# A hybrid decoder layer on eight cores: loads, rings, mLSTM steps and output tiles moved ahead, and the latent attention's value product streaming the probabilities

## The chip, the cores and the metric

The kernel runs as one program on 8 cores of one Trainium2 chip. Each core takes one of the 8 sequences of the batch and shares nothing with the others. The metric is the device time in microseconds of the slowest core. The kernel before took 2946.66 us in the median of 3 runs (2935.18 to 2951.58).

## What is computed

Each core has `x` of 2048 tokens by 2048 channels, and 256 memory tokens. Cut to what matters:

```
h = rms_norm(x, norm)
m_qk, m_v, m_o, m_z, m_i, m_f, a_cq, a_ckv, a_kr, a_z, c_q, c_z, gates = split(h @ w_in)
# A: mLSTM, 4 heads of 256; q and k from silu(causal conv of 4 taps)
hm = rms_norm(mlstm(mq, mk / 16, mv, m_i, log_sigmoid(m_f))) * sigmoid(m_o) * silu(m_z)
# B: latent attention, 8 heads: 128 plain + 64 rotary channels, values of 128, causal
q = rms_norm(a_cq) @ w_uq;  k_nope, v = split(rms_norm(a_ckv) @ w_ukv);  k_rope = rope(a_kr)
ha = softmax(q @ k.T / sqrt(192), causal) @ v * silu(a_z)
# C: cross attention, 4 heads of 256, into 256 memory tokens
hc = softmax(c_q @ km.T / 16) @ vm * silu(c_z)
merged = sig(g_m) * (hm @ w_br_m) + sig(g_a) * (ha @ w_br_a) + sig(g_c) * (hc @ w_br_c)
out = rms_norm(x + merged @ w_out, final_norm)
```

## The kernel before

Everything is bf16 on TensorE with f32 sums. The normed input stands transposed in two tiles `hT` (tokens 0 to 1023 and 1024 to 2047). Intermediate results go to scratch tensors in DRAM (`MQT`, `MG`, `AZ`, `HAT` and so on) and are loaded from there by the stage that needs them.

**How the order comes about.** `FW.op` and `FW.dma` (L121, L132) record each instruction on its engine at once, in the order of the Python calls, with semaphore waits for what it reads and overwrites. Every engine works strictly in that order. SyncE (SP) issues all loads and stores of activations, GpSimd (POOL) all weight loads. `FW.store` (L91) puts a store on a list, and it is issued 12 TensorE instructions later (`LAG`), or earlier when its tile is to be overwritten or its tensor is read by a load whose stores are not all out. The arena hands freed memory to the next tile, which then waits for the last users of it. `mix` (L250) advances two generators so that both shares of work proceed in proportion; each `yield` tells how many matmuls' worth was done. A *dense* stream, matmuls of 512 columns from the input projection, so fills TensorE beside a *light* stream with short dependent steps.

**The stages in order.** First the norm, transposes and values (to about 166 us). Then the q and k projection with the convolution on VectorE (to about 423 us). Then the output gates of mLSTM heads 0 and 1 (`oz_block`, L698) beside `side` (L877): rotary key and gates (`ki_stream`), latent query norm (`lat_stream`), query projections (`uq_rope`, `uq_nope`). `ki_stream` reads the bias `bif`, and `oz_block` the norm weight `gmh`; both are loaded when that stage begins. The twelve `t16` tiles serve all of these, gate tiles and copies in turn (`copy_out`, L787).

Then the light stream takes `mlstm` (L902), `mla` (L1167) and `cross` (L1285), one after the other, and the dense stream `beside_mlstm` and `beside_attention`.

`mlstm` has 32 steps of 128 tokens for two heads at a time. A step is a row of small functions, spread over five phases with dense matmuls between: `sA` scores and transposes of k, `sB` weighting on VectorE (`PT` the masked scores, `kw` the weighted keys), `sC` and `sD` the state update, `sE` its copy to bf16, `sF` the output, `sG` to `sI` its norm (`hmt`), `sJ` and `sK` the transpose back. `loads` fetches `bm`, `mk`, `mq`, `mv` and `mg` of two steps.

`mla` goes over 8 heads, 4 blocks of 512 queries and, of each block, the key tiles up to the diagonal: 320 items. An item has two score matmuls (`qn` with `kn`, `qr` with `kr`), the exponential on ScalarE into `Pa`, the mask on VectorE, and up to four value matmuls. These hold 128 queries of `Pa` in the array and stream `vx`, whose 129th column gives the sum:

```python
for qt in range(q_lo, 4 * qb + 4):
    fw.op("pe", lambda e: e.matmul(bo, lhsT=P[:, jj * 128:(jj + 1) * 128], rhs=vx[:, kt, 0:129], ...
```

The four outputs of a block lie in banks 2 to 5. At its end VectorE takes each one's reciprocal (`stB`), multiplies by it and by the gate `az` into `hat`, and TensorE transposes `hat` back into `haT`. The stream stands until the whole first block of the `AZ` gates is computed (`all_az0`), and loads `az` for a head at a time.

**The end.** `gated` (L1397) computes one gate and one branch product for 128 output channels and 512 tokens, 16 + 8 matmuls. 13 of 16 shares of the first branch run in the dense stream (`first_share`); the rest, and the output projection, run alone, for the two halves of the tokens (`th`). The output projection (L1541 on) has 32 units of 16 matmuls. A unit adds its 512 columns to a tile `xo` that holds 128 rows of `x`; after four units of a tile, `finish` scales it and stores it. There are two `xo` tiles, loaded again for each pair. Between pairs 0 and 1 of the first half, the whole `HT` is loaded back into `hT[0]` (4 MB in one DMA) and `hb2` with it; `hb0` and `hb1` follow when the output weights in them are used up.

## Time and profile before

| | |
|---|---|
| median of 3 runs | 2946.66 us |
| the profiled execution | 2922.08 us |
| its span, slowest core (core 5) | 2921.0 us |
| spans of the eight cores | 2886.8 to 2921.0 us |
| mean granted TensorE clock, core by core | 0.977 to 0.981 |
| PE busy | 2707.9 us, 93% |
| PE weight loads busy | 1305.9 us, 45% |
| DVE busy | 937.9 us, 32% |
| ACT busy | 772.3 us, 26% |
| POOL busy | 399.7 us, 14% |

All are of one profiled execution, but for the first row. The span runs from the first to the last instruction of a core. Busy time is the union of an engine's instructions. Matmuls are pipelined, so the length given for one (380 ns) is not its price: a run of 16 with 512 columns takes 3.45 us. PE is TensorE's matmuls, DVE is VectorE, ACT is ScalarE, POOL is GpSimd. The kernel's slowest core is not far from the others, and both dies have the same clock.

### The profile page before, as it was taken

What the parts mean: (1) busy time and instruction counts of PE and PEld (TensorE: products, weight loads), DVE (VectorE), ACT (ScalarE), POOL (GpSimd) and SP (SyncE); (2) the same over time, 40 slices, a digit from 0 to 9 for tenths busy, and PEclk for the clock granted to TensorE, in tenths of its full rate; (3) what the DMA queues carried; (4) which work ended last, traced back from release to release, by engine and by line L of the source; (5) the groups of instructions that cost most, each with busy time, mean ns of one, the idle gap of its engine ahead of it and who ended that gap; (6) DMA issues with size and microseconds to landing.
All of it is one profiled execution on the core that took longest, in us unless ns stands there. A gap on an engine that the chain in (4) does not pass through costs nothing.

```text
span 2921.0 us, 42383 instructions; the slowest of 8 cores (2886.8 to 2921.0 us)
## 1 busy us (share of the span) xinstructions
PE 2707.9 (93%) x14237; PEld 1305.9 (45%) x14237; DVE 937.9 (32%) x1778; ACT 772.3 (26%) x1551; POOL 399.7 (14%) x566
## 2 busy tenths in 40 slices
PE   5999998988899999799999989999997899999997
PEld 2545443433444444355555544444443444444443
DVE  3455763354544433233322242111121211111123
...
GB/s 258 167 87 166 97 103 72 19 112 96 96 112 67 156 142 121 125 60 132 124 65 98 104 193 197 128 114 138 120 88 215 205 76 76 78 75 77 65 116 144
DMA packets 186580, 342.02 MB, mean 117 GB/s; under 512 B 46272, under 2 KB 140800, under 8 KB 176128
## 3 DMA queue, kind: packets, MB, share of 16 engines
...
## 4 chain that ended last, share of the span: by engine, by line
PE 80%; DMA 11%; DVE 4%; issue 2%; ACT 2%; SPq 1%; POOL 1%; DVEq 0%; ACTq 0%; POOLq 0%
PE bk L1401 21%; PE bk L460 20%; PE bk L449 13%; PE bk L1409 10%; PE bk L1559 5%; PE bk L1239 2%; PE bk L1210 2%; PE bk L1212 2%; DMA out<-m_xo 2%; DMA m_wgb<-wGB 1%; DMA ACC<-m_tmpc 1%; DMA MG<-m_t 1%; DMA m_bif<-bif 1%; DMA m_mv<-MV 1%; DMA m_cq<-CQT 1%
## 5 line engine op out<-in xcount | busy, mean ns | idle before, releaser
L460 PE MATMUL bk<-m_w,m_hT 128*128 128x512 bf16 x3072 | 731.2, 384 | 14.1 <-DVE m_t L740 10.0
L1401 PE MATMUL bk<-m_hT,m_wgb 128*128 128x512 bf16 x3072 | 708.5, 380 | 3.4 <-DMA m_wgb<-wGB 3.4
L1401 PEld LDWEIGHTS bk<-m_hT,m_wgb 128*128 128x128 bf16 x3072 | 299.0, 98 | 355.2 <-issue 7.7
L460 PEld LDWEIGHTS bk<-m_w,m_hT 128*128 128x128 bf16 x3072 | 299.8, 99 | 349.1 <-issue 31.4
L1409 PE MATMUL bk<-m_hb,m_wgb 128*128 128x512 bf16 x1536 | 369.4, 381 | 12.7 <-DMA m_hb<-HMT 7.5
L449 PE MATMUL bk<-m_hT,m_w 128*128 128x512 bf16 (+1 forms) x1600 | 366.9, 382 | 14.0 <-ACT m_t L791 7.2
L1414 DVE SCALAR_TENSOR_TENSOR m_tmpc<-m_sg,bk 128x512 f32<-128x512 f32 x160 | 109.8, 688 | 653.3 <-PE bk L1401 423.3
L1406 ACT ACTIVATE m_sg<-bk 128x512 f32<-128x512 f32 x192 | 114.8, 598 | 768.7 <-PE bk L1401 714.2
L449 PEld LDWEIGHTS bk<-m_hT,m_w 128*128 128x128 bf16 (+1 forms) x1600 | 156.7, 99 | 200.4 <-issue 27.6
L1409 PEld LDWEIGHTS bk<-m_hb,m_wgb 128*128 128x128 bf16 x1536 | 150.0, 98 | 192.1 <-issue 17.4
L1215 ACT ACTIVATE m_Pa<-bk 128x512 bf16<-128x512 f32 (+1 forms) x320 | 168.8, 534 | 248.3 <-PE bk L1212 149.3
L1239 PE MATMUL bk<-m_vx,m_Pa 128*128 128x129 bf16 x1088 | 119.4, 220 | 27.2 <-DVE m_stB L1259 22.0
L140 POOL DMA_DIRECT2D m_wgb<-wGB x96 | 53.2, 555 | 600.7 <-PE bk L1210 323.5
L1559 PE MATMUL bk<-m_wo,m_mergedT 128*128 128x512 bf16 x512 | 113.6, 382 | 20.0 <-DVE m_xo L1566 20.0
L1239 PEld LDWEIGHTS bk<-m_vx,m_Pa 128*128 128x128 bf16 x1088 | 85.5, 98 | 102.3 <-issue 44.1
L1210 PE MATMUL bk<-m_qn,m_kn 128*128 128x512 bf16 (+1 forms) x320 | 111.4, 348 | 4.1 <-ACT m_Pa L1215 3.9
L679 DVE SCALAR_TENSOR_TENSOR m_ybuf<-m_pre,m_cw,m_ybuf 128x2048 f32<-128x2048 f32 x48 | 112.9, 2351 | 5.4 <-DVE m_ybuf L676 0.5
L1559 PE MATMUL bk<-m_hb,m_mergedT 128*128 128x512 bf16 x512 | 111.8, 379 | 1.2 <-DVE m_xo L1566 1.2
L1518 POOL TENSOR_TENSOR m_mergedT<-m_acc,m_tmpc 128x512 bf16<-128x512 f32 x64 | 80.7, 1260 | 233.1 <-DVE m_tmpc L1414 233.1
L1212 PE MATMUL bk<-m_qr,m_kr 128*128 128x512 bf16 (+1 forms) x320 | 111.5, 348 | 0.0
L1569 ACT ACTIVATE m_sg<-m_xo 128x512 bf16<-128x512 f32 x64 | 40.4, 632 | 219.7 <-DVE m_xo L1566 216.8
L1146 DVE SCALAR_TENSOR_TENSOR m_t<-m_t,bk 128x512 bf16<-128x512 f32 x64 | 43.9, 687 | 147.0 <-PE bk L460 91.4
...
## 6 DMA issues: line engine op xcount, KB each, us to landing
m_wgb<-wGB POOLq DMA_DIRECT2D x96, 768.0 KB, 7.7
m_w<-wA POOLq DMA_DIRECT2D x16, 2048.0 KB, 19.7
m_xt<-x SPq DMA_DIRECT2D x16, 1024.0 KB, 12.9
m_xo<-x SPq DMA_DIRECT2D x16, 1024.0 KB, 5.6
out<-m_xo SPq DMA_DIRECT2D x15, 1024.0 KB, 5.8
m_w<-wMEM POOLq DMA_DIRECT2D x4, 2048.0 KB, 16.8
...
m_accl<-ACC SPq DMA_DIRECT2D x16, 512.0 KB, 7.0
```

The costliest lines, as they stand in the source:

```text
L449: fw.op("pe", lambda e: e.matmul(bk[0:M, 0:n], lhsT=w[:, kc, c0:c0 + M], rhs=src(kc, tb * 512, n), start=(kc == 0), stop=(kc == KC - 1)), ...
L460: fw.op("pe", lambda e: e.matmul(bk[:, 0:ncols], lhsT=src(kc, tt * 128, 128), rhs=w[:, kc, 0:ncols], start=(kc == 0), stop=(kc == KC - 1)) ...
L679: fw.op("dve", lambda e: e.scalar_tensor_tensor(out=yb[:], in0=pre[:, tap:tap + S], scalar=cw[:, j, tap:tap + 1], in1=yb[:], op0=ALU.mult, ...
L1210: fw.op("pe", lambda e: e.matmul(bs[:, 0:ncols], lhsT=kn[:, kc_], rhs=qn[:, q0:q0 + ncols], start=True, stop=False), reads=[kn.r, qn.r], w ...
L1212: fw.op("pe", lambda e: e.matmul(bs[:, 0:ncols], lhsT=kr[:, kc_], rhs=qr[:, q0:q0 + ncols], start=False, stop=True), reads=[kr.r, qr.r], w ...
L1215: fw.op("act", lambda e: e.activation(out=P[:, 0:ncols], in_=bs[:, 0:ncols], func=AF.Exp, scale=SC), reads=[r_bs], writes=[P.r])
L1239: fw.op("pe", lambda e: e.matmul(bo, lhsT=P[:, jj * 128:(jj + 1) * 128], rhs=vx[:, kt, 0:129], start=(kt == 0), stop=(kt == qt)), reads=[P ...
L1401: fw.op("pe", lambda e: e.matmul(gb[:, 0:512], lhsT=w[:, kc, :], rhs=h0[:, kc, tcs], start=(kc == 0), stop=(kc == 15)), reads=[w.r] + h0.r ...
L1406: fw.op("act", lambda e: e.activation(out=sg, in_=gb[:, 0:512], func=AF.Tanh, scale=0.5), reads=[r_gb], writes=[r_sg])
L1409: fw.op("pe", lambda e: e.matmul(rb[:, 0:512], lhsT=w[:, 16 + kc, :], rhs=hb[:, kc, tcs], start=(kc == 0), stop=(kc == 7)), reads=[w.r, hb ...
L1414: fw.op("dve", lambda e: e.scalar_tensor_tensor(out=o[:], in0=sg, scalar=1.0, in1=rb[:, 0:512], op0=ALU.add, op1=ALU.mult), reads=[r_sg, r ...
L1559: fw.op("pe", lambda e: e.matmul(bk[:, 0:512], lhsT=mT[:, kc, t8 * 128:(t8 + 1) * 128], rhs=wv[:, kc, :], start=(kc == 0), stop=(kc == 15) ...
```

## The change

- `store` takes a lag of its own and keeps its list sorted by due time.
- `bif` and `gmh` are allocated and loaded in the convolution stage, after the second projection block's second tile (`early_loads`).
- The output gates get a ring of their own, `g16` (6 tiles of 256 columns, lag 28). `t16` has 11 tiles, and 8 from the last dense block beside the mLSTM on.
- In the mLSTM `kw` goes ahead of `PT`; `sG` moves to the end of its own step, `sH` and `sI` a phase earlier, `loads` two phases earlier; a second `loads` stands at the start. A phase counts 3.61 rather than 3.53.
- The `AZ` gates are computed channel by channel instead of token by token (`az_block`), so `AZ` lies transposed, and a head waits only for its own tiles.
- In `mla` the value matmul holds 128 keys of `vx` in the array and streams up to 512 queries of `Pa`; the output comes out transposed, in banks 2 and 3 in turn. The sums are added up on VectorE (`sumP`), split into two bf16 parts (`hi`, `lo`), and summed over the partitions by two matmuls with `twos`. One row of the result goes to DRAM (`DEN`), comes back as 32 x 16 (`dn`) for the reciprocal, goes out again (`REC`) and comes back on all partitions (`rec`), and GpSimd multiplies. This is the generator `closing`, which goes on over 11 items beside the next block. Scores run 3 items ahead, not 2, on four banks.
- The output projection gets four `xo` tiles with a semaphore entry per 512 columns, a table of hooks that says after which unit each load is issued, and `HT` in 8 pieces.

```diff
+        def early_loads():
+            fw.dma("sp", bif[:], bif_d, writes=[bif.r])
+            fw.dma("sp", gmh[:], gmh_d, writes=[gmh.r])
...
+                if h == 1 and ci == 1:
+                    early_loads()
...
-        t16s, nxt_t16 = mk("t16", 12, [128, 512], BF16)
+        t16s, nxt_t16 = mk("t16", 11, [128, 512], BF16)
+        g16s, nxt_g16 = mk("g16", 6, [128, 256], BF16)
...
             loads(0)
+            loads(1)
...
                 if ok(t - 1):
                     sD(t - 1, 1)
-                    sG(t - 1)
+                    sH(t - 1)
                 if ok(t):
                     sA(t)
                 yield 1
                 if ok(t - 1):
-                    sH(t - 1)
                     sE(t - 1, 1)
                 if ok(t):
                     sB(t)
-                yield 1
                 if ok(t - 1):
                     sI(t - 1)
+                    if t % 2 == 0 and 0 < t and t + 2 < N:
+                        loads(t // 2 + 1)
+                yield 1
...
                     sE(t, 0)
-                    if t % 2 == 0 and t + 2 < N:
-                        loads(t // 2 + 1)
+                    sG(t)
...
+            def closing(h, qb, acc, u):
+                k = 4 * h + qb
+                hi, lo = nxt_hi(), nxt_lo()
+                fw.op("act", lambda e: e.copy(out=hi[:], in_=acc[:]), reads=[acc.r], writes=[hi.r])
+                fw.op("dve", lambda e: e.tensor_tensor(out=lo[:], in0=acc[:], in1=hi[:], op=ALU.subtract), reads=[acc.r, hi.r], writes=[lo.r])
+                yield 3
+                bd, r_bd = q_banks()
+                for part in (hi, lo):
+                    fw.op("pe", lambda e: e.matmul(bd[:, 0:512], lhsT=twos[:], rhs=part[:], start=(part is hi), stop=(part is lo)),
+                          reads=[twos.r, part.r], writes=[r_bd])
+                rec = nxt_rec()
+                fw.op("act", lambda e: e.copy(out=rec[0:1, :], in_=bd[0:1, 0:512]), reads=[r_bd], writes=[rec.r])
+                fw.store(DEN_d[k:k + 1, :], rec[0:1, :], reads=[rec.r], to=m_DEN[k])
+                yield 3
+                dn = nxt_dn()
+                fw.dma("sp", dn[:, 0:16], DEN_d[k:k + 1, :].rearrange("o (p c) -> (o p) c", c=16), reads=[m_DEN[k]], writes=[dn.r])
+                yield 3
+                fw.op("dve", lambda e: e.reciprocal(out=dn[:, 16:32], in_=dn[:, 0:16]), reads=[dn.r], writes=[dn.r])
+                fw.store(REC_d[k:k + 1, :].rearrange("o (p c) -> (o p) c", c=16), dn[:, 16:32], reads=[dn.r], to=m_REC[k])
+                yield 1
+                fw.dma("sp", rec[:], REC_d[k:k + 1, :].partition_broadcast(128), reads=[m_REC[k]], writes=[rec.r])
+                yield 1
+                haT = nxt_haT()
+                fw.op("pool", lambda e: e.tensor_tensor(out=haT[:], in0=u[:], in1=rec[:], op=ALU.mult), reads=[u.r, rec.r], writes=[haT.r])
+                fw.store(HAT_d[h * 128:(h + 1) * 128, qb * 512:(qb + 1) * 512], haT[:], reads=[haT.r], to=m_HA[qb // 2])
...
+                if kt == 0:
+                    while h not in az_heads:
+                        yield 1
+                    az = nxt_az()
+                    fw.dma("sp", az[:], AZ_d[h * 128:(h + 1) * 128, qb * 512:(qb + 1) * 512], reads=[m_AZ[h]], writes=[az.r])
...
+                fw.op("pe", lambda e: e.matmul(bo[:, off:512], lhsT=vx[:, kt, :], rhs=P[:, 0:ncols], start=(kt == 0), stop=(kt == last)),
+                      reads=[P.r, vx.r], writes=[r_bo])
...
+                    fw.op("dve", lambda e: e.tensor_tensor(out=acc[:, off:512], in0=acc[:, off:512], in1=P[:, 0:ncols], op=ALU.add),
+                          reads=[P.r, acc.r], writes=[acc.r])
...
+                    fw.op("dve", lambda e: e.tensor_tensor(out=u[:], in0=bo[:, 0:512], in1=az[:], op=ALU.mult), reads=[r_bo, az.r], writes=[u.r])
...
+            for u, t8 in ((0, 2), (0, 3), (9, 4), (10, 5), (17, 6), (18, 7)):
+                at(u, x_load, xos[t8 % 4], th * 8 + t8)
+            if th == 0:
+                for q in range(8):
+                    at(2 + 3 * q, h0_piece, q)
+                for i in range(4):
+                    at(14 + 4 * i, fetch_gb, 48 + i)
+                at(26, load_hb, hb0, 0, 1)
+                at(28, load_hb, hb1, 1, 1)
...
+            if th == 0:
+                ar.free(xos[2:])
+                del xos[2:]
+                hb2 = ar.alloc("hb", [128, 8, 1024], BF16)
+                load_hb(hb2, 2, 1)
```

How the change moves instructions is shown at three places. A number at a row's start only counts rows.

VectorE in the mLSTM, one step (rows with `m_t` are the dense stream's gate evictions). Before:

```order
439 L998 SCALAR_TENSOR_TENSOR m_Cf<-m_Cf,m_eb,bk 128x257 x2
440 L1030 TENSOR_SCALAR m_stM<-m_stM 128x2
441 L1033 SCALAR_TENSOR_TENSOR m_stM<-m_stM 128x2
442 L970 TENSOR_TENSOR m_PT<-bk,m_DT 128x256
443 L976 TENSOR_SCALAR m_kw<-bk,m_WS 128x256 x2
444 L705 SCALAR_TENSOR_TENSOR m_t_3430<-m_t_3430,bk 128x256
445 L707 SCALAR_TENSOR_TENSOR m_t_3430<-m_t_3430 128x256
446 L709 TENSOR_TENSOR m_t_3438<-m_t_3430,m_gmh 128x256
447 L1042 SCALAR_TENSOR_TENSOR m_hmt<-bk,m_stM,m_mg 128x256 x2
```

and now:

```order
439 L1012 SCALAR_TENSOR_TENSOR m_Cf<-m_Cf,m_eb,bk 128x257 x2
440 L1044 TENSOR_SCALAR m_stM<-m_stM 128x2
441 L1047 SCALAR_TENSOR_TENSOR m_stM<-m_stM 128x2
442 L721 SCALAR_TENSOR_TENSOR m_t_3435<-m_t_3435,bk 128x256
443 L723 SCALAR_TENSOR_TENSOR m_t_3435<-m_t_3435 128x256
444 L725 TENSOR_TENSOR m_g_3450<-m_t_3435,m_gmh 128x256
445 L988 TENSOR_SCALAR m_kw<-bk,m_WS 128x256 x2
446 L991 TENSOR_TENSOR m_PT<-bk,m_DT 128x256
447 L1056 SCALAR_TENSOR_TENSOR m_hmt<-bk,m_stM,m_mg 128x256 x2
```

`kw` stands ahead of `PT`, the statistics `stM` a phase before them, and `hmt` directly behind `PT`, with no eviction between.

SyncE's DMAs in the attention, one head change, where `kn` to `vx` are the next head's. Before:

```order
414 L140 DMA HAT<-m_haT 128x1024
415 L140 DMA m_kn<-KNT 128x2048
416 L140 DMA m_qn<-QNT 128x2048
417 L140 DMA m_qr<-QRT 64x2048
418 L140 DMA m_vx<-VA 128x16x128
419 L140 DMA m_az<-AZ 128x16x128
420 L140 DMA CZ<-m_t_3434 128x512
```

and now:

```order
454 L144 DMA DEN<-m_rec 1x512
455 L144 DMA m_kn<-KNT 128x2048
456 L144 DMA m_qn<-QNT 128x2048
457 L144 DMA m_qr<-QRT 64x2048
458 L144 DMA m_vx<-VA 128x16x128
459 L144 DMA m_dn<-DEN 32x16
460 L144 DMA CZ<-m_t_3439 128x512
461 L144 DMA DEN<-m_rec 1x512
462 L144 DMA REC<-m_dn 32x16
463 L144 DMA m_rec<-REC 128x512
464 L144 DMA m_dn<-DEN 32x16
465 L144 DMA HAT<-m_haT 128x512
```

Between the head's loads and the dense stream's stores (`CZ`) now stand the small DMAs of two closings.

GpSimd from the end of the mLSTM on; `m_w` and `m_wgb` are weights. Before:

```order
232 L1035 TENSOR_TENSOR m_stM<-m_stM,m_mhalf 128x2 x2
233 L140 DMA m_w<-wA 128x8192 x2
234 L140 DMA m_wgb<-wGB 128x3072 x20
235 L1515 TENSOR_TENSOR m_acc<-m_accl,m_tmpc 128x512 x2
```

and now:

```order
232 L1049 TENSOR_TENSOR m_stM<-m_stM,m_mhalf 128x2
233 L144 DMA m_w<-wA 128x8192
234 L1277 TENSOR_TENSOR m_haT<-m_u,m_rec 128x512 x6
235 L144 DMA m_w<-wA 128x8192
236 L1277 TENSOR_TENSOR m_haT<-m_u,m_rec 128x512 x8
237 L144 DMA m_wgb<-wGB 128x3072 x4
238 L1277 TENSOR_TENSOR m_haT<-m_u,m_rec 128x512 x9
```

The weight loads stood together with nothing between; now each group comes after multiplications of earlier blocks.

## Rows read from the trace of the kernel before

**Rows 1.** Stretches: us, busy time (and instructions) of each engine, PEclk, DMA share, GB/s

```profile
690.00:1182.00 492.00, 446.02 (x2457) 221.74 (x2458) 215.93 (x515) 190.17 (x503) 99.32 (x149) 0.98 0.51 111
1182.00:1680.00 498.00, 463.52 (x3064) 247.19 (x3063) 140.38 (x484) 208.21 (x391) 6.96 (x13) 0.98 0.45 101
...
2150.00:2300.00 150.00, 121.27 (x547) 53.69 (x545) 37.74 (x39) 22.88 (x63) 11.71 (x33) 0.92 0.67 197
```

**Rows 2.** Timeline, gates' start: start, us, what; in brackets the idle time before

```profile
459.23 0.68 ACT L734 ACTIVATE m_gif<-bk,m_bif 8x512 f32<-8x512 f32 x1 [28.33 <-DMA m_bif<-bif]
...
462.34 8.00 PE L460 MATMUL bk<-m_w,m_hT 128*128 128x512 bf16 x28 [10.03 <-DVE m_t L740]
```

**Rows 3.** PE's waits from 600 to 690 us: us in total, times, longest

```profile
PE bk L449 <- ACT m_t L791: 10.5, 1, 10.5
```

**Rows 4.** Pieces of the chain that ended last: start, us, what

```profile
629.97 30.12 DMA MG<-m_t
...
973.01 15.53 DMA m_bm<-BH
...
1195.89 14.60 DMA AZ<-m_t
...
1226.06 0.23 PE bk L1239 x4
...
2304.52 3.45 PE bk L1401 x16
...
2791.44 110.52 PE bk L1559 x512
```

**Rows 5.** PE's waits in the mLSTM, from 690 to 1182 us

```profile
PE bk L986 <- DVE m_kw L976: 15.2, 12, 2.5
PE bk L449 <- ACT m_t L791: 7.2, 4, 5.5
PE bk L1051 <- DVE m_hmt L1042: 6.5, 6, 2.2
PE bk L986 <- DMA m_mv<-MV: 4.1, 1, 4.1
PE bk L986 <- DVE m_Cf L998: 4.1, 3, 3.4
```

**Rows 6.** PE's waits in the attention, from 1182 to 1680 us

```profile
PE bk L1239 <- DVE m_stB L1259: 22.0, 24, 15.3
PE bk L1210 <- ACT m_Pa L1215: 3.9, 8, 0.6
PE bk L1239 <- DVE m_hat L1261: 3.7, 12, 0.3
```

**Rows 7.** Groups by form: busy us, mean ns of one, idle before

```profile
L1146 DVE SCALAR_TENSOR_TENSOR m_t<-m_t,bk 128x512 bf16<-128x512 f32 x64 | 43.9, 687 | 147.0 <-PE bk L460 91.4 <-PE bk L1239 26.0 <-PE bk L1272 10.9
```

**Rows 8.** DMAs issued from 1315 to 1335 us: KB each, us to landing

```profile
m_wgb<-wGB POOLq DMA_DIRECT2D x4, 768.0 KB, 30.5
m_w<-wA POOLq DMA_DIRECT2D x1, 2048.0 KB, 17.9
...
CZ<-m_t SPq DMA_DIRECT2D x2, 128.0 KB, 16.8
```

**Rows 9.** The same of the whole execution, median landing

```profile
out<-m_xo SPq DMA_DIRECT2D x15, 1024.0 KB, 5.8
...
AZ<-m_t SPq DMA_DIRECT2D x32, 128.0 KB, 1.8
...
m_vx<-VA SPq DMA_DIRECT2D x8, 512.0 KB, 9.5
...
m_hb<-HMT SPq DMA_DIRECT2D x2, 2048.0 KB, 9.4
```

**Rows 10.** PE's waits from 2150 to 2300 us

```profile
PE bk L1559 <- DVE m_xo L1566: 21.2, 3, 17.6
PE bk L1409 <- DMA m_hb<-HMT: 7.5, 1, 7.5
```

283 lines of the change are left out of this document (150 added, 133 removed).

## The prediction, made before the change was run

> **What bounds the kernel now.** I read the table of stages first. Its columns to look at are PE's busy time against the stretch and the granted clock: TensorE is busy 446 of 492 us while the mLSTM runs, 464 of 498 us during the latent attention, and only 121 of 150 us in the output projection of the first half, at a clock of 0.92 [rows 1]. Nothing else comes near a stage's length: VectorE is busy 140 us of the attention's 498. So time can only come from TensorE's idle stretches, and for each I looked up what ended it.
>
> At the gates' start ScalarE waits 28.33 us for the 8-element bias `bif`, and TensorE stands for 10.03 us. The 28 matmuls after that take 8.00 us [rows 2], where 16 of them take 3.45 at full clock [rows 4], so 28 should take 6.0: a long stop costs some 2 us more at half clock. I charge these 2 us wherever PE stops for long.
>
> In the query projection PE waits 10.5 us once for ScalarE's `t` tile [rows 3]; the chain names the `MG` store that holds the tile, 30.12 us long [rows 4].
>
> In the mLSTM the waits are many and small: 15.2 us for `kw`, 6.5 for `hmt`, 7.2 for an eviction, 4.1 for `mv` and 4.1 for the state [rows 5]. The eviction's longest wait stood behind the load of `bm`, 15.53 us [rows 4].
>
> At the attention's start one wait of 15.3 us ends with VectorE's first reciprocals [rows 6]; the chain shows the `AZ` store of 14.60 us behind it [rows 4]. Over the stage the block ends cost 22.0, 3.9 and 3.7 us, that wait included [rows 6]. In the output stage PE waits 21.2 us for `xo` tiles and 7.5 for `hb` [rows 10]. The same 512 matmuls of the second half run in 110.52 us without a stop [rows 4].
>
> **The change part by part.**
>
> *Early `bif` and `gmh`.* Both loads go ahead of the last queue of weights, into the conv stage, which has time. That takes away 10.0 + 2.0 = **12 us** (bounds 8 and 12; nothing new is waited for).
>
> *Own ring for the gate tiles, lag 28.* The `t16` ring loses its 64 gate tiles to `g16` and has 11 buffers left for the copies. The 30 us in which stores land late [rows 4] stay, since two weight loads are under way. A copy comes every 1.7 us (4 of its matmuls and 4 of the gates', 8/16 of 3.45), so 11 buffers last 19 us where 12 shared ones last 17. I take **3 us** of the 10.5 (bounds 0 and 10).
>
> *mLSTM.* `kw` goes ahead of `PT`, and the statistics, `hmt` and the loads a phase or two earlier. `kw` gains one VectorE operation only, but has no statistics of the same phase before it: I take 9 of 15.2. `hmt` has a whole phase more: 6 of 6.5. The loads stand two phases earlier, some 6 us (492 us in 165 phases), against waits of 5.5, 4.1 and 3.4 at most: 10 of these 13. Together **25 us**. The bounds are 0 (the evictions of the dense stream, which stand between these steps, hold them as before) and the whole 37 [rows 5].
>
> *Attention's start.* Each head waits only for its own four tiles of `AZ`, and the mLSTM's share of the mix grows from 3.53 to 3.61, so head 0's tiles are long stored: 15.3 + 2 = **17 us** (bounds 12 and 17).
>
> *Block ends.* With the sums streamed over 512 queries there are two output banks in turn, so PE need not wait for evictions: (22.0 - 15.3) + 3.9 + 3.7 = **14 us**. The transposes go too, see the work.
>
> *TensorE's work.* 1088 value matmuls at 0.23/4 us are 62.6 us [rows 4], and 128 transposes of as many columns each are 7. In their place stand 320 matmuls with 139264 columns, which at 3.45 us for 16 x 512 are 58.6, and 64 matmuls for the denominators, 13.8. Net **3 us more**. So streaming by itself saves nothing: weight loads were hidden already.
>
> *VectorE.* 296 running additions of up to 512 columns, and two more operations a block, at 0.69 us at most [rows 7] some 230 us, less 80 us of the old ones. VectorE goes from 140 to 290 us of 498. That lies beside TensorE and costs nothing while it isn't held up.
>
> *The denominators' way.* This is the new wait. Each of 32 blocks makes four DMAs in a row: `DEN` out, `dn` in, `REC` out, `rec` in. VectorE's reciprocal stands three items behind the load of `dn`, 4.5 us (498/320 = 1.5 us an item). An undisturbed small store lands in 1.8 us, so mostly it is there in time. Behind the next head's `vx` it is 9.5 us [rows 9], 5 us too late seven times. But during weight loads small stores landed after 16.8 us, with the loads themselves at 17.9 and 30.5 [rows 8]. VectorE is strictly in order: behind a waiting reciprocal stand the additions that free `Pa` tiles, the masks and the evictions of the dense stream's two banks. A dense unit takes 3.45 us and about as much again of the attention's work, so I let PE outlast some 5 us. POOL now has its multiplications between the weight fetches, which therefore come in three separate groups inside the attention: one 2 MB, one 2 MB, and four of 768 KB together with `hb`. A single one would hold VectorE 17.9 - 4.5 = 13 us at worst; I take 11, so PE 6 and 2 for the clock. The last I take at 22 of 26 us, so PE 17 and 2. Sum 8 + 8 + 19 = **35 us** more. Bounds: 2 (all meet a moment between closings) and 160 (below).
>
> The Trainium skill, page "DMA: Bandwidth & Descriptors", section "Queues, rings and completion order", says that each DMA engine takes turns between the queues, packet by packet, so that a small transfer on one queue has to wait for little of a large one on another. By it these stalls would be near 2 us, and the sum 33 us lower. The trace bears it out badly: behind the weights, issued on another queue, the 128 KB stores took nine times as long as alone [rows 8, 9].
>
> *Output tiles.* Four `xo` buffers, loaded 6 to 8 units of 3.45 us before their use, and `HT` in eight pieces rather than 4 MB in one that blocks the queue. All 28.7 us go, with two half-clock stretches 33. Late next is `hb2`: its load now waits for the stores of the last two tiles. Such a store was issued about 6 us after its tile's last matmul, by the steps of `finish`, and lands in 5.8, and 2 MB of `hb` need 9.4 more [rows 9], 21 us with nothing else under way; it is wanted after four gated blocks of 24 matmuls (5.18 us each) and 16 matmuls more, 24 us. I take 3 us. Gain **30 us** (bounds 20 and 33).
>
> **The sum.** -12 - 3 - 25 - 17 - 14 + 3 + 35 - 30 = **-63 us**. The profiled execution took 2922.1 us, of which 2921.0 are the span, so it would take 2859. It lies 24.6 us under the median of the runs shown, 2946.66, and I take the difference from that: **2884 us**.
>
> **The rivals.**
>
> *A, the round trips stay hidden* (2 in place of 35): 2946.7 - 96 = 2851 us. For it: undisturbed landings of 1.8 us, and `u` and `rec` have two buffers, so only the reciprocal and `u`'s `az` tile can hold VectorE. Against it stand the late stores [rows 8]. The Trainium skill's rule, above, would give this case. Chance 0.27.
>
> *B, the mLSTM keeps its waits* (5 in place of 25) and the round trips cost 50: 2946.7 - 28 = 2919 us. For it: VectorE's rows between the steps of the mLSTM are evictions, and those did not move. Chance 0.13.
>
> *C, slower: the reciprocal holds VectorE at every block.* The place is the wait for `dn`; the price is 5 us of PE in each of 32 blocks, 160 in place of 35: 2884 + 125 = 3009 us. It decides once `dn` lands more than 4.5 + 5 = 9.5 us after its issue as a rule, which is what the landing behind `vx` shows [rows 9]. SyncE is in order too: a `dn` load waits there until `DEN` has landed, and a `rec` load until `REC` has, with stores and head loads queued behind. Against it: of the blocks only one in four stands right behind a head's loads. Chance 0.08.
>
> **How the numbers follow.** My forecast has 0.52. The range from 2830 to 2942 us runs from A with all 37 us of the mLSTM (about 2839, and some spread of the runs, 2935 to 2952 before) to B with the round trips at 70; C and the ends of the others, 2 in 10, are left out. A measurement of this kernel can tell about 0.5%, 14.7 us, from no change. Under 2932 us lie all of A, nearly all of the forecast and two thirds of B: 0.86. Within 0.5% on both sides 0.07, slower 0.07, nearly all C.
>
> **What would show it.** PE's wait at the gates' start gone, and `m_gif` not behind `bif`. In the mLSTM's stretch the five waits [rows 5] at 12 us rather than 37, with `kw` under 8. At the attention's start no wait over 3 us. In the attention two to four stops of PE of 5 to 20 us that end with VectorE, each at a time of weight loads, with `m_dn` or `m_az` as the last releaser; none there would mean A, one at every block C. The 512 output matmuls of the first half in some 112 us, and a stop of a few us at the second half's first use of `hb2`. If the attention's stage lost nothing and the mLSTM's waits only changed their names, the gain would be right by accident.

## The result, and the profile after

The changed kernel took 2978.98 us in the median of 20 runs (from 2944.91), the kernel before 2945.14 in as many beside it. The ratio is 1.0091, with a 95% interval of 1.0053 to 1.0128: **slower by 0.9%**, where 2884 us and 86% for faster had been forecast. (The two medians are of all runs; in the ratios and in the experiments' times, runs in which one half of the chip, cores 0 to 3 or 4 to 7, was held at a lower clock are left out, and for e5 to e8, where almost none would be left, I give the mean core span of the halves that were not held, against 2911.3 us for five such halves of the kernel before.)

The profiled execution has a span of 2943.7 us (before 2921.0), on core 5 again. Cut at the same instructions in both, it splits as follows:

| stretch | before, us | after, us | difference |
|---|---|---|---|
| norm, convolution | 423.7 | 420.4 | -3.3 |
| gates, query projections | 267.0 | 270.2 | +3.2 |
| mLSTM | 504.1 | 496.8 | -7.3 |
| latent attention | 481.6 | 545.7 | **+64.1** |
| cross attention | 96.5 | 101.6 | +5.1 |
| dense work up to the output, first half | 378.3 | 375.7 | -2.6 |
| output, first half | 133.8 | 114.4 | -19.4 |
| dense work, second half | 506.3 | 498.3 | -8.0 |
| output, second half, and end | 129.8 | 120.5 | -9.3 |

The stretches that answer to [rows 1], with the same columns:

```profile
690.00:1187.00 497.00, 457.30 (x2519) 227.18 (x2520) 218.53 (x517) 190.71 (x505) 99.73 (x150) 0.97 0.54 113
1187.00:1733.00 546.00, 453.55 (x2111) 208.09 (x2109) 281.85 (x581) 234.19 (x446) 47.00 (x43) 0.91 0.43 101
2210.00:2325.00 115.00, 112.97 (x516) 50.67 (x515) 35.42 (x38) 22.46 (x62) 11.57 (x33) 0.99 0.84 238
```

The attention has fewer matmuls than before and takes longer, at a mean granted clock of 0.91 where it was 0.98. That mean is not one level but two: pieces at half clock among others at full clock, such as these after the first stop:

```profile
1203.00:1206.00 3.00, 3.00 (x9) 1.03 (x7) 0.21 (x1) 1.32 (x3) 0.00 (x0) 0.50 0.00 0
1207.00:1240.00 33.00, 33.00 (x164) 15.66 (x163) 21.97 (x42) 19.21 (x36) 2.53 (x2) 1.00 0.47 109
```

By the trace's clock record, the stretch has 14 such pieces of 3.4 to 13.7 us, 92.9 us in all, where before had 17.1. The output stage has lost its idle time.

One thing has to be known before stretches are compared. The dense stream is mixed in by counts, and the change altered the counts. Between the first score matmul and the cross attention's first, the traces have 1140 dense matmuls of 512 columns before (764 + 256 + 120) and 1084 now (512 + 240 + 224 + 108); the 56 others stand elsewhere, 44 of them in the dense stretch behind the cross attention and 12 in the mLSTM's. At 3.45 us for 16 they are 12.1 us. So for the same work the attention is not 64 but some 76 us longer. Of the 64.1, TensorE's idle time makes 58.3 (34.2 before, 92.5 now) and its busy time 5.8. By the forecast's own +3 us for the attention's matmuls and the 12.1 us fewer dense ones, the busy time should have fallen by 9, so my estimate of what the half clock cost is 15 us.

TensorE's waits in the attention, which answer to [rows 6], are these (in us: total, times, longest):

```profile
PE bk L1262 <- DVE m_dn L1271: 35.0, 7, 5.6
PE bk L1262 <- DVE m_Pa L1249: 18.7, 2, 10.2
PE bk L1317 <- DMA m_vx<-VA: 10.1, 1, 10.1
PE bk L1262 <- ACT m_hi L1257: 6.1, 3, 3.4
PE bk L1262 <- DVE m_lo L1258: 4.8, 3, 3.0
PE bk L1317 <- DVE m_Pa L1249: 4.2, 1, 4.2
PE bk L1470 <- DVE m_tmpc L1475: 2.8, 1, 2.8
```

L1262 is the pair of denominator matmuls. Together these make 81.7 us, against 29.6 in [rows 6]. One more ends the stretch, the first load of the cross attention (before, 1.2 us):

```profile
PE bk L1368 <- DMA m_cq<-CQT: 10.9, 1, 10.9
```

SyncE had issued that load only at 1729.9 us, right after a store of `haT` for which it had waited 7.2 us.

The releaser in these rows is put down to the instruction that VectorE finished last, so one has to ask what VectorE itself waited for, and then what SyncE waited for:

```profile
DVE m_dn L1271 <- DMA m_dn<-DEN: 57.2, 14, 10.3
DVE m_u L1336 <- POOL m_haT L1277: 34.3, 7, 5.6
...
DVE m_u L1336 <- DMA m_az<-AZ: 29.7, 3, 12.5
```

```profile
SPq L77 <- POOL m_haT L1277: 140.7, 32, 7.2
SPq L77 <- DMA REC<-m_dn: 70.5, 32, 14.3
SPq L77 <- DVE m_dn L1271: 55.5, 28, 5.9
SPq L77 <- DMA DEN<-m_rec: 39.0, 20, 7.1
```

Two things show. The seven waits of 35 us have their like in VectorE's seven waits for GpSimd's `haT`: a block's `u` overwrites that of two blocks earlier, which the multiplication at the end of that block's closing has yet to read. And SyncE stands 306 us of 546 for steps of the closings, with the `az` loads behind them. (The 306 us are no price: in e4 below, which has no way through DRAM, SyncE stands 339 us of 483.) One such piece, from the timeline (start, length, engine; idle time before in brackets):

```profile
1306.11 0.59 POOL L144 DMA_DIRECT2D m_w<-wA  x1 [7.88 <-PE bk L1244]
...
1308.01 1.68 SPq L144 DMA_DIRECT2D REC<-m_dn  x1
1321.57 0.34 SPq L144 DMA_DIRECT2D m_rec<-REC  x1
...
1323.82 0.38 PE L1262 MATMUL bk<-m_hi,m_twos 128*128 128x512 bf16 x1
1325.50 1.25 POOL L1277 TENSOR_TENSOR m_haT<-m_u,m_rec 128x512 bf16<-128x512 f32 x1 [18.80 <-DMA m_rec<-REC]
1326.88 0.34 SPq L144 DMA_DIRECT2D HAT<-m_haT  x1
1327.75 0.44 SPq L144 DMA_DIRECT2D m_az<-AZ  x1
1331.27 0.69 DVE L1336 TENSOR_TENSOR m_u<-bk,m_az 128x512 f32<-128x512 f32 x1 [11.68 <-DMA m_az<-AZ]
1332.71 0.59 PE L1262 MATMUL bk<-m_lo,m_twos 128*128 128x512 bf16 x1 [8.51 <-DVE m_Pa L1249]
```

A 2 MB weight load starts on GpSimd's queue. The 2 KB of `REC`, issued on SyncE's 2 us later, have SyncE wait 11.8 us, until 1321.57 (of the 32 such stores one more took over 7 us, 14.6 us from 1441.5 on, 14 us after four weight loads had been issued); then comes `rec`, the multiplication, the store of `haT`, and only then the `az` load of the current block. VectorE's `u` waits for it, `lo` stands behind `u`, and TensorE is 8.5 us late. The reciprocal has no part in this stop.

Outside the attention two waits took the place of removed ones. At the gates:

```profile
426.46 0.29 POOL L815 TENSOR_SCALAR m_Mneg<-m_maskf 128x128 f32<-128x128 f32 x1 [66.94 <-ACT m_cosT L675]
426.88 0.57 POOL L144 DMA_DIRECT2D m_w<-wKI  x1
...
434.66 1.89 PE L457 MATMUL bk<-m_hT,m_w 128*72 128x512 bf16 x4 [13.24 <-DMA m_w<-wKI]
```

The wait for `bif` [rows 2] is gone. But with `gmh` allocated earlier, the small mask `Mneg` was given the place of a tile that ScalarE still read for the cosine. GpSimd waits there, and the weights `wKI` behind it come 34 us later than before (393.0 us). In the mLSTM, against [rows 5]:

```profile
PE bk L457 <- DVE m_t L1177: 14.7, 2, 12.4
PE bk L1000 <- DVE m_kw L988: 11.1, 9, 3.3
PE bk L969 <- ACT m_hmo L1073: 3.8, 1, 3.8
```

`hmt` and `mv` are waited for no longer, the state for 1.2 rather than 4.1 us, `kw` for 11.1 rather than 15.2, and a new wait of 12.4 us is an `AZ` gate tile's: the `t16` ring, cut to 8 just there, is full of stores that land late behind a weight load.

### The profile page after: what moved, and what is told of

The parts are those of the page before. It is cut to its first block, busy times and chain, and to the rows that moved or that the text cites. A ratio compares the mean times of both kernels' runs of the same rounds, so it can differ in the third digit from the quotient of the medians.

```text
span 2943.7 us, 41762 instructions; the slowest of 8 cores (2900.3 to 2943.7 us)
## 1 busy us (share of the span) xinstructions
PE 2719.1 (92%) x13405; PEld 1278.0 (43%) x13405; DVE 1083.3 (37%) x1881; ACT 802.1 (27%) x1615; POOL 440.2 (15%) x598
## 4 chain that ended last, share of the span: by engine, by line
PE 76%; DMA 15%; DVE 3%; issue 2%; POOL 1%; SPq 1%; ACT 1%; DVEq 0%; POOLq 0%; ACTq 0%
PE bk L1462 20%; PE bk L468 16%; PE bk L457 16%; PE bk L1470 10%; PE bk L1638 8%; DMA m_dn<-DEN 3%; DMA REC<-m_dn 2%; DMA m_rec<-REC 2%; PE bk L1242 1%; PE bk L1244 1%; PE bk L1317 1%; DMA DEN<-m_rec 1%; DMA QNT<-m_t 1%; SPq L144 1%; DMA m_wgb<-wGB 1%
## 5 line engine op out<-in xcount | busy, mean ns | idle before, releaser
L468 PE MATMUL bk<-m_w,m_hT 128*128 128x512 bf16 x2560 | 616.3, 387 | 1.5 <-DVE m_Gt L839 1.5
L457 PE MATMUL bk<-m_hT,m_w 128*128 128x512 bf16 (+1 forms) x2112 | 494.0, 384 | 37.6 <-DVE m_t L1177 14.7
L468 PEld LDWEIGHTS bk<-m_w,m_hT 128*128 128x128 bf16 x2560 | 251.4, 99 | 285.6 <-issue 22.0
L457 PEld LDWEIGHTS bk<-m_hT,m_w 128*128 128x128 bf16 (+1 forms) x2112 | 207.3, 99 | 284.2 <-issue 60.5
L1325 DVE TENSOR_TENSOR m_sumP<-m_sumP,m_Pa 128x512 f32<-128x512 f32 (+3 forms) x264 | 159.1, 603 | 11.7 <-ACT m_Pa L1247 0.3
L1317 PE MATMUL bk<-m_Pa,m_vx 128*128 128x512 bf16 (+1 forms) x320 | 114.7, 359 | 14.2 <-DMA m_vx<-VA 10.1
L1277 POOL TENSOR_TENSOR m_haT<-m_u,m_rec 128x512 bf16<-128x512 f32 x32 | 41.0, 1281 | 483.0 <-DMA m_rec<-REC 390.4
L720 ACT ACTIVATE m_t<-bk 128x512 f32<-128x512 f32 x64 | 38.2, 597 | 209.3 <-PE bk L468 199.8
## 6 DMA issues: line engine op xcount, KB each, us to landing
ACC<-m_tmpc SPq DMA_DIRECT2D x32, 256.0 KB, 11.2
```

Of the source, the lines that this page charges most:

```text
L457: fw.op("pe", lambda e: e.matmul(bk[0:M, 0:n], lhsT=w[:, kc, c0:c0 + M], rhs=src(kc, tb * 512, n), start=(kc == 0), stop=(kc == KC - 1)), ...
L468: fw.op("pe", lambda e: e.matmul(bk[:, 0:ncols], lhsT=src(kc, tt * 128, 128), rhs=w[:, kc, 0:ncols], start=(kc == 0), stop=(kc == KC - 1)) ...
L1317: fw.op("pe", lambda e: e.matmul(bo[:, off:512], lhsT=vx[:, kt, :], rhs=P[:, 0:ncols], start=(kt == 0), stop=(kt == last)), reads=[P.r, vx ...
L1325: fw.op("dve", lambda e: e.tensor_tensor(out=acc[:, off:512], in0=acc[:, off:512], in1=P[:, 0:ncols], op=ALU.add), reads=[P.r, acc.r], wri ...
```

## The experiments

Edits are against the changed kernel, unless they say before. Ratios are to the kernel before on the same chip; "attention" is the length of that stretch in the profiled execution, on its slowest core if none is named.

### Which part costs

**e1** takes the old `mla` and the old `AZ` gates back; **e2** puts only the new ones into the kernel before.

```diff
-            yield from az_block(0, d2_banks)
+            yield from gate_block(I_AZ[0], AZ_d, 0, m_AZ[0], d2_banks)
+            all_az0.append(True)
...
```

> The kernel after with the attention and the AZ gates of before; early loads, rings, mLSTM steps and output tiles stay changed. Theory S (the loss of the change is made inside the attention): its stretch goes back from 546 to about 482 us, the wait of about 15 us for the first reciprocals returns within it, and the whole takes about 64 us less than after: ratio to before 0.985 to 0.992. Rival M (the loss comes from moved arena places and from SyncE's and GpSimd's order, wherever it shows): under a third of the 64 us comes back, ratio over 1.0.

> The kernel before with the new attention and the transposed AZ gates only. Theory S: it loses what e1 gains, about 55 to 65 us, ratio to before 1.019 to 1.022, with the gap between the two denominator matmuls (hi to lo) at some 60 us in total. Rival M: the new attention alone costs under 20 us, ratio under 1.007, and most of the loss of after comes only with the other parts.

e1: 2883.51 us, ratio **0.9817** (0.9789 to 0.9846), attention 483 us. e2: 2981.5 us, **1.0158** (1.008 to 1.0235), attention 534. Theory S holds, and more than expected: without the new attention the change is 1.8% faster. The attention costs 46 us alone (e2, 23 to 69), 64 in its own stretch, 76 there for the same work, and some 80 as the difference of after and e1.

**e8** puts only the output projection's changes into the kernel before, **e14** only the mLSTM's order and 3.61, **e16** only the early loads.

> The kernel before with the output projection's changes alone (four xo tiles with an entry per 512 columns, the table of hooks, HT in eight pieces, hb2 behind). The prediction had 30 us for it (28.7 of waits, two half-clock stretches, less 3 for hb2). In after the stages from the first output projection on were shorter by 19.4 + 8.0 + 9.3 = 36.7 us, of which 9.3 after the last matmul. Theory: the same here, ratio 0.986 to 0.989. Rival: part of that came from the four-way last tile or from other changed places, and alone it gives under 25 us, ratio over 0.991.

The mean span is 2869.8 us (5 halves) against 2911.3 for before. That is -41 us, **0.986**: the theory holds.

> The kernel before with the new order of the mLSTM steps and the phase count of 3.61 only. The prediction had 25 us for it (waits of 37 us down to 12), with 0 as the bound if the dense stream's evictions between the steps hold them as before. In after the stretch was 7.3 us shorter, with a stop of 12.6 us in it that came from the shortened t16 ring. Theory O (the order gives its 25 us, the ring took part of it back): ratio to before 0.991 to 0.994 and the five waits together at 12 to 17 us. Theory N (most waits changed their names only): 0.995 to 0.999, lost time of TensorE in the stretch at 60 us or more against 71.7 before.

0.9992 (0.9954 to 1.0029), nothing. Between the two profiles the stretch shrank by 14.0, 11.2 and 6.6 us on cores 0, 1 and 3 (on core 1 with `kw` at 10.9 and `hmt` at nothing), but the three stretches behind it, up to the output, grew by 11.1, 12.8 and 18.8 us. Over all eight cores the means are -8.4 and +11.0 us. The waits did not only change their names, so N's mechanism is not it; its number comes close, since what was gained there was lost behind. The count of 3.61 has a small part in that: it moves 16 dense matmuls, 3.4 us, out of the attention (1140 to 1124) and behind the cross attention, which makes nothing longer as a whole. But in the attention TensorE's idle time also grew, from a mean of 32.4 to 40.6 us, and no run shows why.

e16's edit:

```diff
+        gmh = ...; bif = ...; Mneg = ...    # ahead of the rotary tables' tiles
+                if h == 1 and ci == 1:
+                    early_loads()
```

> The kernel before with bif and gmh loaded in the convolution stage as in the change, and with Mneg there too, so that GpSimd's queue isn't held as it was in after; no other ring. The prediction had 12 us for the early loads (bounds 8 and 12), and after showed no gain: the wait for wKI (13.4 us) stood where that for bif (10.2) had been. Theory P: with the queue free the 12 us are there, ratio 0.995 to 0.997. Rival: as in e12 against e1 (0.9819 and 0.9817), where the wait of 14.2 us went and the whole took as long; then 0.998 to 1.001.

0.9977 (0.9937 to 1.0018), -7 us in the middle: not told apart from nothing, nor from the 12 us of theory P. The gates' stretch itself did get shorter, from a mean of 266.0 us over the eight cores to 257.5.

**e7** moves `Mneg` the same way in the changed kernel.

> The kernel after with the mask tile Mneg allocated and filled in the convolution stage, ahead of the rotary tables' tiles. In after GpSimd stands 66.9 us before it, because its place was that of a tile which ScalarE still read for the cosine, and the load of wKI stands behind it, issued at 426.9 us instead of 393.0 in before; TensorE then waits 13.4 us for wKI. Theory P (a moved arena place holds GpSimd's queue, and that is all the gates' stage lost): the 13 us wait goes, nothing comes in its place, norm to gates together 12 to 15 us shorter, ratio to before 1.003 to 1.006. Rival (another wait stands behind it, for gmh or for the two weights): under 5 us, ratio 1.007 to 1.012.

No stop at `wKI` is left, and the gates' stretch is 259 us rather than 270 (core 0). The mean span is 2927.7 us (7 halves), 1.006 to before. Theory P, as far as this goes; its number is at the edge.

### Which wait of the closings costs

**e3**:

```diff
-            us, nxt_u = mk("u", 2, [128, 512], F32)
+            us, nxt_u = mk("u", 4, [128, 512], BF16)
```

> The kernel after with four u tiles in bf16 (4 KB) in place of two in f32 (4 KB), so that a block's product u need not wait for GpSimd's multiplication of the block two before; all DMAs and the reciprocal stay where they are. Theory U (VectorE is held by the u ring: 34 us of waits for GpSimd's haT, seven times, once a head): the seven stops of TensorE of 4 to 6 us before the matmul of lo go, 35 us of the 60.6, the two of 9 to 10 us that stand behind a late az load stay; ratio to before about 0.997 (after: 1.009). Theory D (VectorE is held by the reciprocal that waits for dn, as rival C of the prediction had it): nothing changes, 1.009 within 0.003.

1.0006 (0.9979 to 1.0033): a gain of 25 us on the changed kernel, where theory U had 35. The seven stops are gone, theory U holds for them. But VectorE's waits for `dn` grew:

```profile
DVE m_dn L1271 <- DMA m_dn<-DEN: 103.2, 24, 10.1
DVE m_u L1336 <- DMA m_az<-AZ: 31.5, 3, 12.0
```

**e4** computes the same with no way through DRAM:

```diff
-                rec = nxt_rec()
-                fw.op("act", ... copy(out=rec[0:1, :], in_=bd[0:1, 0:512]) ...)
...
+                rec = nxt_rec()
+                fw.op("dve", lambda e: e.reciprocal(out=rec[:], in_=bd[:, 0:512]), reads=[r_bd], writes=[rec.r])
+                yield 1
```

> The kernel after with no way through DRAM: VectorE takes the reciprocal of the denominators straight from the bank, on all 128 partitions (128x512), right behind the two matmuls, and GpSimd multiplies an item later. The four DMAs of a block are gone. Theory Q (SyncE's order is what costs: behind a DEN, REC or rec that waits, az and head loads and stores stand): all of the 60.6 us between the two denominator matmuls go but for a few, less what the reciprocal takes; at 0.7 us a piece, as other 128x512 operations, the attention's stretch is about 480 us and the ratio to before 0.987 to 0.990. If the reciprocal is dear (over 3 us a piece, 96 us of VectorE in all), VectorE holds TensorE again and the ratio stays over 1.0. Theory W (the running sums' 190 us of VectorE are what costs, not the closings): the stretch stays over 520 us either way.

There are two runs, 2889.32 and 2892.69 us, against 2929.11, the median of seven of before: about 0.987, with no interval. The attention takes 483 us. The reciprocal is dear, and the sentence on that case is wrong:

```profile
L1265 DVE RECIPROCAL m_rec<-bk 128x512 f32<-128x512 f32 x32 | 107.3, 3353 | 5.0 <-PE bk L1262 4.9
```

```profile
1185.00:1668.00 483.00, 427.72 (x2048) 199.67 (x2088) 390.78 (x581) 216.14 (x413) 49.24 (x43) 0.96 0.42 97
```

VectorE is busy 391 us of 483 and doesn't bound: TensorE waits 4.1 us for the new reciprocal. The work beside TensorE is harmless here; waits for a DMA, in order, are not. Theory W falls. (This stretch holds 1064 dense matmuls, 20 fewer than after's, 4.3 us: without the closings' long tail fewer are mixed in.)

**e5** (four `u`, and the 32 x 16 reciprocal as a power of -1 on GpSimd), **e6** (four `u`, and `az` loaded a block ahead) and **e9** (both) take the other holders away.

```diff
-                fw.op("dve", lambda e: e.reciprocal(out=dn[:, 16:32], in_=dn[:, 0:16]), ...
+                fw.op("pool", lambda e: e.tensor_tensor(out=dn[:, 16:32], in0=dn[:, 0:16], in1=mone[:], op=ALU.pow), ...
```

```diff
+                    if k + 1 < 32 and (k + 1) // 4 in az_heads:
+                        load_az(k + 1)
```

> As e3 (four u tiles in bf16), and the 32x16 reciprocal is taken by GpSimd (a power of -1) rather than by VectorE, so that VectorE never waits for dn; all four DMAs of a block stay, in SyncE's order. In e3 VectorE waited 103 us for dn in 24 places, up to 10.1 each, and TensorE still stood some 45 us longer in the attention than in e4. Theory D2 (that rest is VectorE behind dn, seen as late m_hi): most of it goes, the stretch falls from 528 to about 490 us and the ratio to before to about 0.988. Theory Q2 (it is SyncE, where az and head loads stand behind DEN, REC and haT): under a third goes, stretch over 512, ratio over 0.995, and the stops behind m_az stay.

> As e3, and the az tile of a block is loaded at the start of the block before, in the same two buffers. Theory Q2: the two stops of 9 us before lo (at about 1320 and 1450 us) and the one of 6.8 beside the second go, some 20 to 25 us, ratio 0.992 to 0.994. Theory D2: the reciprocal still waits and holds VectorE at the same places, so under 8 us go, ratio 0.998 to 1.001.

> e5 and e6 together: four u tiles, the reciprocal on GpSimd, and az a block ahead. The round trip through DRAM stays with its four DMAs. e5 and e6 gave nothing each, and in their traces the wait only changed its name: without dn on VectorE it waited 84.8 us for az, with az early it waited 130.4 us for dn. Theory B (the closings cost only by what they hold on VectorE, and each holder hides the other): with both away the attention's stretch is 480 to 495 us, as in e4 (483), ratio to before 0.985 to 0.990. Theory T (the round trip costs in itself, by SyncE's order for the head loads, the dense stream's stores and the rings, or by GpSimd's 2.9 us for each power): the stretch stays over 515 us, ratio over 0.995.

e5: 2947.6 us (3 halves), 1.012, attention 560 (core 5). e6: 2913.9 us (5 halves), 1.001, attention 529 (core 5). e9: **1.015** (1.0096 to 1.0204), attention 569. The theories with a gain (D2 in e5, Q2 in e6, B in e9) fell; in e6 it came out as D2 had it, no gain and VectorE held by `dn`. e6's stops behind `az` did go, and others came, behind `hi` (43.8 us, 14 times): I take it for the same VectorE, now late through `dn`. One row of each tells it, of e5 (core 5), of e6 (core 5) and, of e9, ScalarE's and TensorE's:

```profile
DVE m_u L1338 <- DMA m_az<-AZ: 84.8, 7, 21.7
```

```profile
DVE m_dn L1278 <- DMA m_dn<-DEN: 130.4, 25, 12.1
```

```profile
ACT m_rec L1274 <- POOL m_haT L1286: 112.7, 11, 14.7
...
PE bk L1251 <- ACT m_rec L1274: 70.5, 10, 11.4
```

With VectorE free of both, ScalarE is held: its copy of the sums goes into one of two `rec` tiles, and the exponentials stand behind it.

**e13** gives e9 rings of three for `u` (e9 has four), `dn` and the sums, which get tiles `den` of their own; `rec` stays at two, and these tiles and `DEN` and `REC` are bf16, for room. And **e15** issues e13's closing DMAs and the `haT` stores on GpSimd.

```diff
-                rec = nxt_rec()
-                fw.op("act", lambda e: e.copy(out=rec[0:1, :], ...
+                den = nxt_den()
+                fw.op("act", lambda e: e.copy(out=den[:], ...
```

```diff
-                fw.dma("sp", dn[:, 0:16], DEN_d[k:k + 1, :] ...
+                fw.dma("pool", dn[:, 0:16], DEN_d[k:k + 1, :] ...
```

> e9 with rings that outlast a closing at every place where an engine writes: the row of denominators gets its own ring of three tiles (den, bf16) in place of the two rec tiles, rec is written by its load only, dn and u have three tiles; DEN and REC lie in bf16. In e9 VectorE was free of both holders and ScalarE stood instead, 112.7 us in 11 places, for GpSimd's multiplication that reads rec, TensorE 70.5 us behind it. Theory R (what costs is the in-order engine held by a ring of two against a round trip longer than a short block; with rings of three none is held): no stop of TensorE over 5 us between 1200 and 1690 us, stretch 478 to 495 us, ratio 0.985 to 0.991. Theory T (the round trip itself costs through SyncE's queue, where it holds head loads and the dense stream's stores): the stops come back under further names (m_t of the dense stream, m_qn, m_kn), stretch over 515, ratio over 1.0.

> e13 with the four DMAs of the round trip and the store of haT issued by GpSimd, so that SyncE's queue holds nothing of the closings; the trip stays the same. In e13 SyncE stood 362 us of 567 for haT, dn, DEN and REC, and VectorE 63 us for az and 49 us for stores of tmpc behind it. Theory T (SyncE's order carries the trip's waits to all other loads and stores): the waits for az and for ACC end, stretch 475 to 495 us, ratio to before 0.983 to 0.991. Rival G (the same in GpSimd's order: its weight fetches wait behind the closings instead, or the trip's length itself holds VectorE on u): stretch over 510 us, with waits of TensorE for m_w or m_wgb, ratio over 0.998.

e13: **1.0177** (1.0084 to 1.027), attention 567 us on the slowest core. Rings aren't enough; SyncE stands as before, and `az`, a whole block ahead, comes up to 24.2 us late. From e13, SyncE's waits and one of VectorE's:

```profile
SPq L77 <- POOL m_haT L1288: 153.1, 31, 14.2
SPq L77 <- POOL m_dn L1281: 122.8, 32, 7.2
SPq L77 <- DMA DEN<-m_den: 44.0, 24, 6.5
SPq L77 <- DMA REC<-m_dn: 42.4, 32, 4.8
```

```profile
DVE m_u L1351 <- DMA m_az<-AZ: 63.4, 5, 24.2
```

e15: **1.0312** (1.0253 to 1.0371), attention 577 to 595 us over the cores. SyncE no longer waits for the trip, and `az` comes in time, but now GpSimd takes every landing, its 2.9 us power and the multiplication one after the other, and VectorE waits for the `u` ring of three:

```profile
DVE m_u L1351 <- POOL m_haT L1288: 170.5, 18, 27.8
```

That is rival G's second form: the length of the trip itself. So e15 says nothing on SyncE alone. **e17** is e4 with `u` in bf16 and one `rec` tile; **e18** adds the four DMAs, of a row that nobody reads (edit against e17):

```diff
+                fw.store(DEN_d[k:k + 1, :], rec[0:1, :], reads=[rec.r], to=m_DEN[k])
...
+                fw.dma("sp", dn[:, 0:16], DEN_d[k:k + 1, :] ..., reads=[m_DEN[k]], writes=[dn.r])
+                yield 3
+                fw.store(REC_d[k:k + 1, :] ..., dn[:, 0:16], reads=[dn.r], to=m_REC[k])
+                yield 1
+                fw.dma("sp", jr[:], REC_d[k:k + 1, :].partition_broadcast(128), reads=[m_REC[k]], writes=[jr.r])
```

> The partner of e18, on the same chip: e4 (reciprocal straight from the bank) with u in bf16 and one rec tile, which makes room for e18's unused tile. All theories: as e4, stretch of the attention 478 to 488 us, ratio to before 0.984 to 0.989.

> e17 with the four DMAs of the round trip issued by SyncE as in after, 3 items apart and each waiting for the one before, but with nothing that computes waiting for them: a row of rec goes to DEN, comes back as dn, goes to REC, comes back on 128 partitions into a tile that nobody reads. VectorE, ScalarE and GpSimd do what they do in e17. Theory T (SyncE's order alone carries the loss): az, head loads and stores behind the trip come late, the stretch is 25 us or more longer than e17's, ratio 0.994 or more. Theory H (the loss needs an engine that waits for the trip's result, VectorE for dn and u): SyncE stands for DEN and REC as before, 110 us or so, but the stretch is within 10 us of e17's, ratio under 0.991.

e17: 0.9902 (0.9869 to 0.9935), attention 469 to 479 us over the cores, mean 475.1. e18: 0.9984 (0.9944 to 1.0023), attention 489 to 498, mean 493.3. That lies between the two theories: the trip in SyncE's order costs 18 us of the stretch, of which 4.3 are 20 dense matmuls more (1084 against 1064), and some 24 of the whole, by two ratios whose intervals nearly touch. It is not quite free of engines that wait: with one `rec` tile, VectorE stood once, 9.5 us, for the `DEN` store that reads it (core 3). So 14 us are an upper bound for SyncE's order alone in the stretch. e3 has a mean of 524.2 us, 47 over e4's 476.9; less the same 4.3 us for the matmuls and those 14, nearly 30 us are left for the engines that wait for the result. I can't split that further: each removal changed the other waits.

### What beats both

**e10** is e4 with `az` a block ahead and `Mneg` early. **e11** adds the full `t16` ring (room from `u` in bf16 and one `rec`), and more dense work between a stage's first loads and their use:

```diff
-            ar.free(t16s[8:])
-            del t16s[8:]
...
-            yield 16
+            yield 44
...
-            yield 6
+            yield 24
```

**e12** is e1 with `Mneg` early.

> e4 (reciprocal straight from the bank, no DMAs) with az a block ahead and Mneg in the convolution stage. In e4 the stops left by these are 12.9 us before lo at 1432 us and 14.4 us for wKI at 424: both go, 25 to 29 us off e4's 2889 us, so 2860 to 2866 us, ratio to before 0.976 to 0.979. If the reciprocal of 3.35 us takes their place as holder of VectorE, under 10 us go in the attention and the ratio is 0.982 to 0.985.

> e10, and: u in bf16 and one rec tile, whose room lets the t16 ring keep its 11 tiles; 44 rather than 16 columns' worth of dense work between a head's first loads and the first scores, 24 rather than 6 before the cross attention's. Aimed at the stops of 10.8 us at 1113 (VectorE's gate eviction waits for a store behind a weight load, with a ring cut to 8), 12.1 at 1189 (vx) and 9.6 + 4 in the cross attention (cq). If each was a stop that nothing else stands behind, 30 to 36 us less than e10, ratio 0.965 to 0.970. Rival: the dense work put there is missing at the end of the mix and the stores still land late behind the weights: under 12 us less, ratio over 0.973.

> e1 (after with the attention of before) with Mneg in the convolution stage: the 14.2 us wait for wKI goes, 2870 us, ratio to before 0.976 to 0.979. Rival: another wait takes its place, as wKI's took that of bif: 2880 us or more, ratio 0.980 to 0.983.

e10: 0.9807 (0.9737 to 0.9878), of two runs, 2875.28 and 2876.61 us; attention 466. Both stops went, but stops elsewhere grew (11.4 us at an eviction at 1002 us). e12: 0.9819 (0.9765 to 0.9874), 2879.56 us, like e1: the 14 us wait is gone, and the ratio is the rival's, but the interval holds the theory's 0.976 to 0.979 too. e11: **0.9733** (0.9675 to 0.9791), median 2851.18 us, attention 453:

```profile
1183.00:1636.00 453.00, 431.71 (x2100) 200.94 (x2099) 386.90 (x580) 214.55 (x413) 46.43 (x44) 0.99 0.42 101
```

That is 28.4 us less than before's 481.6 on the same cut, but it is not what streaming the probabilities is worth. e11's stretch holds 1076 dense matmuls against 1140, 13.8 us that stand elsewhere, and TensorE is idle for 21.3 us rather than 34.2, since the first reciprocals' wait is gone. What is left is 1.7 us. That fits the prediction's sentence that streaming by itself saves nothing. And where the rest is alike, e10 with the new attention (0.9807) and e12 with the old (0.9819) can't be told apart. What e11 has over e10, the full `t16` ring and the dense work ahead of the first uses, I haven't tried on the old attention, so it is not shown that the fastest kernel here needs the new one.

## Why the prediction was wrong

**The sum.** It had -63 us; the span moved by +22.7. By its terms (in the last column, the ratio of the run with that part alone, taken on 2930 us):

| step | forecast | in the profile after | alone |
|---|---|---|---|
| early `bif`, `gmh` | -12 | 0 | e16: -7 (-18 to +5) |
| gate tiles' ring | -3 | -2 | |
| mLSTM | -25 | -7 | e14: -2 (-13 to +8) |
| attention (-17 -14 +3 +35) | +7 | +64, for the same work +76 | e2: +46 (23 to 69) |
| output and its ends | -30 | -37 | e8: -41 |

(The last is the sum of the three lower rows of the stage table. Of the 10.5 us in [rows 3] a wait of 8.6 for the same ring is left. In no term are the cross attention's +5.1 us and the dense stretch's -2.6, which holds 44 matmuls more, 9.5 us.)

**The step that failed** is "so only the reciprocal and `u`'s `az` tile can hold VectorE", and with it 35 us for the closings and 14 gained at the block ends. I had counted two buffers of `u` as enough without laying the closing's length beside the blocks'. A closing goes on over 11 items, and its multiplication stands one item before the end of the second block behind it, the short ones of 4 and 8 items of a new head. Any delay of the trip holds `u` there, once a head: seven waits, 34.3 us, taken away by e3. Second, `az` is loaded when its own block starts, on a queue that I had called "in order too" but priced at nothing: 29.7 us of VectorE's waits. The cross attention's first load, 10.9 us late, stood on the same queue. Third, I had looked for one holder and multiplied; e5, e6, e9 and e13 show five (`u`, `dn`, `az`, `rec`, and SyncE before them), each hidden by the one before it.

In size, the way through DRAM cost 55 us of the stretch rather than 35: the mean over the cores is 535.8 us with it and 476.9 without (e4), less 4.3 for the 20 matmuls. And without it e4 is still some 15 us longer than before for the same work (476.9 against 478.5 us, with 76 dense matmuls fewer, 16.4 us), where the sum's other terms, -17 - 14 + 3, had 28 us less. In e4's profile stops of 12.0 us for `vx`, 12.8 behind `az` and 9.4 for the cross attention's first load stand in the place of that gain. In e11, where none of them is over 4 us, half of it is there: 450.6 us with 64 dense matmuls fewer is 14 us less than before.

**The rivals.** C, the slower one (0.08), had the right kind: an in-order engine held by the trip. Its place was wrong (the reciprocal waited in 14 blocks of 32, and in e3 in 24, for 103 us, and TensorE outlasted most of it) and its 160 us too high. The signs given for it, "one at every block", did not appear. For A little speaks: most of the 32 `REC` stores of 2 KB did land in 1.3 us or little more, but two held SyncE 11.8 and 14.3 us beside weight loads on another queue. The Trainium skill, page "DMA: Bandwidth & Descriptors", section "Queues, rings and completion order", says that each DMA engine takes turns between the queues, packet by packet. That such a wait is then short, near 2 us, was the prediction's own inference, and these two stores don't agree with it; whether the turns are taken as the page says, these rows can't show.

**The attention's start** was right that the first reciprocals' 15.3 us would go, and wrong in "no wait over 3 us": `vx` takes 10.1 us in its place. It is the same 2 MB weight load that holds another transfer now. Before, it was issued 15 us after `vx`, which had landed, and it was the `AZ` store behind it that took 14.60 us [rows 4]; now it is issued 0.6 us after `vx` (at 1179.93 us), which is awaited until 1201.28:

```profile
1194.63 0.62 POOL L140 DMA_DIRECT2D m_w<-wA  x1 [27.84 <-PE bk L460]
```

```profile
1180.54 0.62 POOL L144 DMA_DIRECT2D m_w<-wA  x1 [15.29 <-PE bk L457]
1201.28 0.58 PE L1317 MATMUL bk<-m_Pa,m_vx 128*128 128x512 bf16 x1 [10.06 <-DMA m_vx<-VA]
```

**Early loads.** "Nothing new is waited for" failed: the arena hands out places by order of allocation, and the moved `gmh` moved `Mneg`.

**The mLSTM.** The mechanism was partly right (`hmt` to 0, as foretold; `kw` to 11 us, foretold under 8), but e14 shows that the whole gains nothing. Adding a stage's gain to the sum assumes that the other stages stay as they are.

**The output** was right, even low. The forecast had 28.7 us of waits and 4 for the half clock, less 3; the stage gained 19.4 us, and the dense work of the second half, which begins with the `hb` wait, 8.0. Missed was the end, 9.3 us. With one semaphore entry a tile, each scaled piece of the last tile waited for the store of the piece before; the chain of before ends in alternation:

```profile
2914.52 2.30 DMA out<-m_xo
...
2916.91 0.75 DVE m_xo L1494
```

and now the four stand in one go:

```profile
2937.57 2.74 DVE L1556 SCALAR_TENSOR_TENSOR m_xo<-m_xo,m_stO,m_gfin 128x512 f32<-128x512 f32 x4 [2.82 <-POOL m_stO L382]
```
